# Four changes of order and place in an expert kernel: the gather queue, the last residual add and its stores

## The reference

```python
x = x + gt_a * _rms_norm(mix, p['g_post_mix'])            # x1
h2 = _rms_norm(x, p['g_pre_ffn']) * (1.0 + sc_f) + sh_f
f = _hier_moe(h2, ...)     # top-1 group of 4, then top-2 of its 8 experts
x = x + gt_f * _rms_norm(f, p['g_post_ffn'])              # the output y
```

## Time and profile before

| what | us |
|---|---|
| median of three executions | 1982.55 |
| lowest, highest | 1980.0, 1987.84 |
| the profiled execution, its own time | 1980.0 |
| the profiled execution, span from its first to its last instruction | 1978.1 |

### The profile page before, as it was taken

The page is one execution under the profiler, slowest core; times in us unless marked ns, Lnnn a source line. Parts: engine busy times, 40 slices in busy tenths (PEclk is TensorE's granted clock), DMA queues, the critical chain, the costliest instruction groups (busy, mean ns, idle before and its releaser), DMA issues.

```text
span 1978.1 us, 24188 instructions
## 1 busy us (share of the span) xinstructions
PE 1770.5 (90%) x8882; PEld 1399.7 (71%) x8882; DVE 1276.6 (65%) x1624; ACT 1035.4 (52%) x1414; POOL 294.6 (15%) x284
## 2 busy tenths in 40 slices
PE   3799988999999989999999996399999999999980
PEld 0566645666666679999999894278877888777860
DVE  4302236777877773454645645589889899888954
ACT  2413334554555562343544533177777777777844
POOL 0000001222222000000000000013323334323311
PEclk9899988999999999999999998599999999999995
DMA  9463230111111256363555446379998999889839
GB/s 354 171 242 117 75 91 4 36 46 46 46 46 47 72 172 182 124 218 127 181 189 181 160 167 236 115 284 381 375 378 360 365 371 374 349 357 380 350 128 263
DMA packets 92567, 403.70 MB, mean 204 GB/s; under 512 B 14679, under 2 KB 39415, under 8 KB 76088
## 3 DMA queue, kind: packets, MB, share of 16 engines
q1 hardware_dynamic: 76192, 375.80, 50.7%
q0 software_dynamic: 11136, 21.65, 3.5%
q10 hardware_dynamic: 5160, 5.18, 0.8%
HBM read 375.66 MB, written 46.81 MB: 214 GB/s over the span
## 4 chain that ended last, share of the span: by engine, by line
PE 65%; DVE 15%; DMA 10%; ACT 4%; issue 4%; SPq 1%; ACTq 0%; POOLq 0%; DVEq 0%; POOL 0%
PE ps L1654 62%; DMA wg<-w_gate 6%; DVE wd_low L1580 2%; DMA fy<-y_dram 2%; DVE wg_low L1580 1%; ACT wg_up L1060 1%; PE ps L1794 1%; DVE olst L1302 1%; DVE mx L1251 1%; PE ps L1952 1%; DVE xc L1274 1%; PE ps L1984 1%; DMA wraw<-w_ga 1%; DMA nsink<-sinks 1%; DVE xc L1293 1%
## 5 line engine op out<-in xcount | busy, mean ns | idle before, releaser
L923 ACT ACTIVATE wup<-wraw 128x1024 fp32r<-128x1024 f32 x120 | 126.6, 1058 | 260.2 <-PE ps L1654 191.1
L1357 DVE TENSOR_TENSOR wlow<-wraw,wup 128x1024 fp32r<-128x1024 f32 x120 | 146.5, 1224 | 169.8 <-ACT wup L923 169.5
L1654 PE MATMUL ps<-hT,wA 128*128 128x352 f32 x624 | 195.9, 471 | 12.1 <-ACT hT L780 12.0
L1654 PE MATMUL ps<-hT,wB 128*128 128x352 f32 x624 | 189.2, 459 | 0.5 <-ACT gB L867 0.5
L1580 DVE TENSOR_TENSOR wg_low<-wg,wg_up 128x2048 fp32r<-128x2048 f32 x68 | 152.8, 2289 | 43.3 <-ACT wg_up L1060 43.3
L1654 PEld LDWEIGHTS ps<-hT,wA 128*128 128x128 f32 x624 | 120.3, 195 | 81.2 <-ACT hT L780 12.3
L1580 DVE TENSOR_TENSOR wu_low<-wu,wu_up 128x2048 fp32r<-128x2048 f32 x68 | 155.6, 2289 | 16.0 <-ACT wu_up L1065 16.0
L1654 PEld LDWEIGHTS ps<-hT,wB 128*128 128x128 f32 x624 | 118.4, 190 | 64.1 <-issue 1.9
L1580 DVE TENSOR_TENSOR wd_low<-wd,wd_up 128x2048 fp32r<-128x2048 f32 x68 | 152.8, 2288 | 12.4 <-ACT wd_up L1070 12.3
L1060 ACT ACTIVATE wg_up<-wg 128x2048 fp32r<-128x2048 f32 x68 | 126.4, 1908 | 39.2 <-DMA wg<-w_gate 39.2
L1065 ACT ACTIVATE wu_up<-wu 128x2048 fp32r<-128x2048 f32 x68 | 130.0, 1914 | 23.6 <-PE ps L1654 23.5
(11 more groups left out here) (316 smaller groups left out, 4182.9 us busy)
## 6 DMA issues: line engine op xcount, KB each, us to landing
wg<-w_gate SPq DMA_DIRECT2D x34, 2048.0 KB, 12.8
wu<-w_up SPq DMA_DIRECT2D x34, 2048.0 KB, 13.6
wd<-w_down SPq DMA_DIRECT2D x34, 2048.0 KB, 8.5
wada<-w_ada SPq DMA_DIRECT2D x12, 2048.0 KB, 10.9
wraw<-w_ga SPq DMA_DIRECT2D x24, 512.0 KB, 3.6
wraw<-w_gr SPq DMA_DIRECT2D x24, 512.0 KB, 3.6
wraw<-w_at SPq DMA_DIRECT2D x24, 512.0 KB, 3.6
wraw<-w_lr SPq DMA_DIRECT2D x24, 512.0 KB, 3.6
```

The costliest lines, as they stand in the source:

```text
L923: act.activation(wup[n % UP][:, :, :], wraw[n % RAW][:, :, :], ACT.Copy).then_inc(w_rounded, 1)
L1357: V.tensor_tensor(wlow[n % RAW][:, :, :], wraw[n % RAW][:, :, :], wup[n % UP][:, :, :].bitcast(F32), ALU.subtract).then_inc(w_split, 1)
L1654: return pe.matmul(out, lhsT, rhs, start=start, stop=stop, skip_group_check=True)
```

## The change

Four things are changed. (1) On GpSimd's queue the gather ahead of scatter(n) is that of block n+2 instead of block n+3, and one more is issued in all. (2) x1 is stored to a buffer of its own in HBM, `x1_dram`. (3) SP loads x1 back into SBUF (`x1f`, 9 tiles, over the place of the experts' buffers) after the last up projection and the last gathers and before it waits for the last scatters. (4) The last addition, x1 to the scaled tile, is done by GpSimd for tiles 0 to 6 and by VectorE for tiles 7 and 8, and SP stores the sums to `y` by nine plain DMAs.

```diff
+DVE_ADDS = 2
...
+        x1f = at("x1f", [P, TILES, D], e0)
...
+        x1_dram = nc.dram_tensor("x1_dram", [TOK, D], F32)
...
             def x1_store(t, j, n):
                 sp.wait_ge(x1_ready, t + 1)
-                sp.dma_start(O["y"][t * P:t * P + n, :], x1[j][0:n, :]).then_inc(st_x1, 16)
+                sp.dma_start(x1_dram[t * P:t * P + n, :], x1[j][0:n, :]).then_inc(st_x1, 16)
...
+            sp.wait_ge(up_done, 2 * more + 4)
+            sp.sem_inc(idx_seen, 1)
+            for s in range(2):
+                sp.wait_ge(xg_ready[s], 16 * more + 32)
+                sp.sem_inc(idx_seen, 1)
+            sp.wait_ge(st_x1, 16 * TILES)
+            sp.dma_start(x1f[:, 0:BLKS, :], x1_dram[0:SEQ, :].rearrange("(t p) n -> p t n", p=P)).then_inc(ld_x1, 16)
+            sp.dma_start(x1f[0:NS, BLKS, :], x1_dram[SEQ:TOK, :]).then_inc(ld_x1, 16)
+
             for s in range(2):
                 sp.wait_ge(st_y[s], 16 * more + 16)
                 sp.sem_inc(idx_seen, 1)
...
-            sp.wait_ge(y_added, 16 * TILES)
-            sp.wait_ge(st_x1, 16 * TILES)
-            sp.wait_ge(st_out, 16)
+            for t in range(TILES):
+                n = P if t < BLKS else NS
+                if t < TILES - DVE_ADDS:
+                    sp.wait_ge(yo_ready, t + 1)
+                else:
+                    sp.wait_ge(yo_last, t + 1 - (TILES - DVE_ADDS))
+                sp.dma_start(O["y"][t * P:t * P + n, :], fy[0:n, t, 1, :]).then_inc(st_out, 16)
+            sp.wait_ge(st_out, 16 * TILES + 16)
...
             gather(0, 0, 1)
             gather(1, 1, 2)
-            pool.wait_ge(xg_used, 2)
-            gather(2, 0, 3)
-            with pool.Fori(0, more) as i:
+            with pool.Fori(0, more + 1) as i:
                 for s in range(2):
-                    gather(2 * i + s + 3, 1 - s, 4 * i + 2 * s + 4)
-                    scatter(2 * i + s, s, 4 * i + 2 * s + 5)
-            for s in range(2):
-                scatter(2 * more + s, s, 4 * more + s + 4)
-            pool.wait_ge(xg_ready[0], 16 * more + 32)
-            pool.sem_inc(idx_seen, 1)
-
-            pool.wait_ge(st_x1, 16 * TILES)
-            for t in range(TILES):
-                n = P if t < BLKS else NS
+                    gather(2 * i + s + 2, s, 4 * i + 2 * s + 3)
+                    scatter(2 * i + s, s, 4 * i + 2 * s + 4)
+
+            for t in range(TILES - DVE_ADDS):
+                n = P
+                if t == 0:
+                    pool.wait_ge(ld_x1, 32)
                 pool.wait_ge(f_norm, t + 1)
-                pool.dma_start(O["y"][t * P:t * P + n, :], fy[0:n, t, 0, :], accum_op=ALU.add).then_inc(y_added, 16)
+                pool.tensor_tensor(fy[0:n, t, 1, :], fy[0:n, t, 0, :], x1f[0:n, t, :], ALU.add).then_inc(yo_ready, 1)
...
                 V.scalar_tensor_tensor(fy[0:n, t, 0, :], fy[0:n, t, 0, :], fst[0:n, t, 1:2], G2[0:n, :],
                                        ALU.mult, ALU.mult).then_inc(f_norm, 1)
+                if t >= TILES - DVE_ADDS:
+                    dve.wait_ge(f_norm, t + 1)
+                    dve.wait_ge(ld_x1, 32)
+                    V.tensor_tensor(fy[0:n, t, 1, :], fy[0:n, t, 0, :], x1f[0:n, t, :], ALU.add).then_inc(yo_last, 1)
```

More of the change, by code:

```diff
@@ L394, in build @@
         st_y = [sem("st_y0"), sem("st_y1")]
-        st_x1 = sem("st_x1")
+        st_x1, ld_x1 = sem("st_x1"), sem("ld_xf")
         ch_moe, ch_fin2 = sem("ch_moe"), sem("ch_fin2")
@@ L399, in build @@
         ld_f = [sem(f"ld_f{t}") for t in range(LF)]
-        f_first, f_sum, f_sq, f_norm = sem("f_first"), sem("f_sum"), sem("f_sq"), sem("f_norm")
-        y_added = sem("y_added")
+        f_first, f_sum, f_sq, f_norm, yo_ready = sem("f_first"), sem("f_sum"), sem("f_sq"), sem("f_norm"), sem("yo_ready")
+        yo_last = sem("yo_last")
         st_out = sem("st_out")
```

## The result

The changed kernel takes 2003.41 us (median of 6 runs, 1998.56 to 2009.68) against 1982.74 us for the kernel before (6 runs): a ratio of 1.0105, 95% interval 1.0088 to 1.0122, 20.7 us slower. Its profiled execution took 2002.22 us around a span of 2000.4.

A forecast was written before the change was run, and what follows sets the result against it. The prediction took the loop to be bound by TensorE, with DMA close behind, and the tail's chain by `fy` transfers. Loop +22 and tail +4 gave +26 us, a 2008 us median; eight times in ten 1985 to 2032.

The forecast's parts named there:

- The sum: Whole kernel: loop +22 and tail +4 make +26 us, 2006 us for a run like the profiled one, 2008 for the median.
- The forecast case: Whole kernel: slower, 1995 to 2022 us, as gathers land late in the loop and the tail costs more; chance 0.60.
- The loop, +22 us: Expert loop: 31 windows each gain a 1.15 us wait for gathered rows, 594.9 us against 572.7.
- Late weights absorbed, -13.5: Expert loop: longer windows give the weights more time, so 13.5 us of late-weight waits vanish.
- Waits that pull each other even: Expert loop: two neighbouring waits total 2.3 us and even out near 1.15, since after a short window the gather lands later.
- The first rival: Expert loop: waits alternate between 0 and 2.3 us and the clock falls, +43 us, median near 2030; chance 0.17.
- Why the gather is late: GpSimd's queue in the loop: queued behind the scatter, issued at 7.1 us, landing 12.8 later, 1.9 us too late.
- The second rival: Expert loop: the gather lands within about 19 us and stays hidden, 0 to +5 us, total 1980 to 1990; chance 0.15.
- The extra gather at nothing: End of the loop: the two last gathers, one more than before, cost nothing because GpSimd is idle there.
- The tail, +4 us: After the loop: GpSimd's additions take turns with VectorE at 1.9 us each, ending at 1982 against 1978.1 us.
- The third rival: Tail gains 8 us without accumulating stores and engine exclusion, loop loses nothing, 1974 us; chance of faster 0.08.

## Why the prediction was right, step by step

- **The sum.** 2008 us predicted, 2003.41 measured, and 2006 against 2002.22 for the profiled execution. Of the 4 us, 3.6 lie ahead of the first window, whose beginning varies by 8 us between profiles. The forecast case came in, by the mechanism that was named; that the numbers meet so closely is in part luck, as the next two points show.
- **The loop, +22 us.** Measured +22.0 (594.69 against 594.9). The sum is right, but two of its parts are off by 8 us each and cancel. Idle time is 27.2 us, or 0.88 a window instead of 1.15, since the gathers landed 19.86 us after the last block's end and not 20.3. The rest, 8.25 us over 31 x 18.04, is TensorE's busy time, which the sum had at nothing above 18.04 a window: windows with a wait show 18.30 us busy at full clock, and one shows 19.69. Where those 0.26 us come from wasn't tried. With the 567.4 to 575.9 us that the old order's loop takes in its five profiles, the difference would be anything from 19 to 27 us.
- **Late weights absorbed, -13.5.** This term was mis-sized. The waits for `act_h` did go, but they were only 9.3 of the 13.5 us; the other 4.2 were TensorE's busy time (563.41 over 31 x 18.04), and that grew to 8.25 us and wasn't absorbed.
- **Waits that pull each other even.** They lay between 0 and 1.75 us but for one of 2.45 us. They weren't even: seven windows began with no wait, and ended with one of 1.2 to 1.8 us. What kept nearly all of them short is that two neighbouring waits are 1.7 us together on average, and not 2.3. The reason that the prediction gave, a gather that lands later after a short window, would have pushed the waits apart, and it isn't what the trace shows: the gather landed 19.7 us after the last block's end in the seven windows that began with no wait, and 20.4 us in the eight that began with more than 1.4. The one wait of 2.45 us was followed by the clock's lower level. The three microseconds after it in the changed kernel, columns as above:

```profile
1354.00:1357.00 3.00, 3.00 (x12) 2.41 (x11) 1.22 (x1) 2.35 (x2) 1.50 (x3) 0.53 1.00 426
```

  Its window has a mean clock of 0.91 and costs 1.4 us in busy time. The first rival was at work in one window, not in half of them.
- **Why the gather is late.** The prediction named the place behind the scatter, and the kernel with the gather in front shows that this is the cause. But it took the latency of 12.8 us for fixed and the issue for what moves. The runs show a landing that follows the landing of the transfer in front, some 6 us behind it: issued 0.3 us behind the end of the scatter's instruction or after a copy between the two, it comes at +19.8 to +20.0. Issue plus latency gave the right sum since the trace of before had its gathers behind a scatter too; it would have failed for the gather in front, where both shrink. The second rival's condition ("a landing 1.3 us earlier") is what the scatter without its data meets, and the windows then do cost nothing.
- **The extra gather at nothing.** Nearly: it holds back the x1 load by 3 us, and so puts the load beside the last scatter.
- **The tail, +4 us.** Measured +4.0 in the profile, on nearly the steps named: x1 load issued 27.6 us after the last window's beginning (28 predicted), scatter +0.7 (taken: 1), turns of 1.90 us seven times (1.9 predicted; the 1.4 us that the working took off for reciprocals and gaps were not there, 4.48 us a tile against 2.59), the eighth load of `fy` 11.7 us instead of 18.92, first `f_norm` instruction to the end 38.9 us (39.7 by the working). The last down product took 8.53 us at a granted clock of 0.65 against 7.40 at 0.77, which wasn't in the sum. The tail alone, though, measures 0.9999: of the 4 us, 2.3 are the tail's own by the profile, too little to be seen in the times, and 1.7 came with the order.
- **The third rival** needed a gather under 18.5 us and additions that stop VectorE for less than 0.7 us. They were 19.86 and 1.90. Its first half exists: 13.5 us lie in the accumulating stores by the profile, as the kernel without additions shows.

The Trainium skill's rule on the shared port (SBUF — State Buffer, Who interferes with whom) holds to the instruction here: 3.18 us against 1.28 with GpSimd's addition running, 1.28 without it. The Trainium skill's figure of about 2.6 cycles an element (GPSIMD Engine Reference, Elementwise — side-by-side cycle accounting) made my estimate 2.2 us for an addition, and the trace agrees: from the end of VectorE's instruction at 1963.96 to the end of GpSimd's at 1966.16 it is 2.20 us. VectorE lost less, 1.90 us a turn.

## What to carry to other kernels

On a queue that runs in order, look at what each transfer stands behind, not only at how far ahead it is fetched: the transfer that is wanted soonest goes in front of the one that must wait for the last result. A transfer's latency read from a trace holds for its place in the queue, and may change when it is moved: here it fell from 15.0 to 11.0 us in front of the scatter. Emptying the transfer in front helps less than passing it: with an emptied scatter the gather landed 1.5 us sooner (just enough in this loop), in front of the scatter 5.4 us sooner. When two traces are compared, the same load of each is compared, the second with the second and the eighth with the eighth. Before work with two inputs is given to GpSimd to relieve VectorE, compare the pace of the pair with that of VectorE alone; here the help cost more (1.90 us) than the work (1.23 us).

## What the runs showed of the hardware that was not expected

- In this loop a gather of 512 KB right behind a scatter on GpSimd's queue (1.3 to 2.1 us by the medians) lands 14.8 to 15.7 us after its issue, one in front of it after 11.0 us (medians). Whichever of the two is second lands some 6 us after the first. A scatter that writes at most one row still takes 10.2 us to land, so its data explain only about 1.5 us of the gather's delay.
- The indirect DMA instruction itself took 1.02 to 1.05 us in some places and 2.17 to 3.12 us in others. In the kernel before, all 31 long ones of the loop (2.23 to 2.60 us) were issued while VectorE ran `wd_low`, with two inputs in SBUF, and all 31 short ones while it ran `x_low`, which has one of its inputs in PSUM. That fits, but it was not isolated by a run.
- Accumulating stores slow the loads beside them more than plain stores of the same size do: the eighth load of `fy` (1 MB) took 18.9 us beside them, also when only four were left, and 10.8 us beside plain stores.
